# Down product with 25 instead of 18 units of seven products, and with its side work at positions written out in tables

## The chip, the cores and the metric

The kernel runs on one core of a Trainium2 chip. The metric is the device time of one execution in microseconds; the median of several executions is compared. PE is TensorE, DVE VectorE, ACT ScalarE, POOL GpSimd, SP SyncE (it only issues DMAs here).

## The reference

A decoder trunk of two layers over 256 tokens of width 2048, in float32: each layer is an attention part (layer 0: windowed attention with sinks and stick-breaking attention side by side; layer 1: dilated attention) and then a SwiGLU part, each with RMS norm in front and a residual behind. The part at issue is the last line of the SwiGLU:

```python
def swiglu(h, w_gate, w_up, w_down):
    return (jax.nn.silu(h @ w_gate) * (h @ w_up)) @ w_down
```

with `w_gate`, `w_up` of 2048 x 5632 and `w_down` of 5632 x 2048. The product with `w_down` is the **down product**; it runs twice, once for each layer.

## The kernel before

**Splitting.** A float32 product is made of three PE matmuls in a rounded format: both sides are split into a high and a low part, and `three` (L2049) issues high x high, high x low and low x high. ACT makes the high part of a piece of weights (`split`, L1303: `w_hi`, a rounded copy of `raw`), DVE the low part (`split`, L1615: `w_lo` = `raw` - `w_hi`). The prepared pieces ("halves") live in a ring of four slots (`SPLIT` = 4): ACT may write half h+4 only when PE has used half h. The walk through the program gives, on step h, PE its half h, ACT the split of half h+3 and DVE the split of half h+2 (`AHEAD` = 3), and then the other work of that step, in the order in which it is written.

**Eights and sevens.** The down product takes the 44 contraction tiles of 128 in 22 pairs, in two passes over 1024 output columns each (`p` = 0, 1). A pair is a block product of 2 x 2 blocks (two tiles by two halves of the tokens, against two tiles by two column groups of 512). As an "eight" it is done plainly: 8 block products, 24 matmuls of 512 columns, in two halves of 12. As a "seven" it is done after Strassen and Winograd with 7 block products, 21 matmuls, in four parts of 6, 3, 6 and 6 matmuls (`seven_part`, L2055). For that it needs sums of weights (`make_sums`, L1625: three DVE instructions, of 1024, 512 and 512 columns) and forms of the activations (`make_forms`, L1994: four DVE instructions of 128 columns in three steps; `form_high`, L1592, on ACT; `form_low`, L2017, on DVE). Its four parts take splits of 1024, 512, 1024 and 1024 columns ("two", "one", "sums_a", "sums_b"). At the end of a pass, or behind its last seven, the accumulators are mixed on DVE.

**Staging.** The activations of each pair are themselves split into `stage_hi` (ACT, `stage_high`, L1597) and `stage_lo` (DVE, `stage_low`, L1988), 512 columns each, in a ring of four pairs (`STAGED`). In the profile these tiles appear under the names `xT_hi` and `xT_lo`, because they are views of them; the forms appear as `silu_g`.

**Order.** `down` (L824) walks the halves of a pass. Which pairs are sevens stands in `DOWN_SEVENS` (L49): pairs 7, 11, 14, 18, 21 in the first pass and 9, 12, 15, 18 in the second, in both layers. On each step, after the split and after the work of `first_pass` or `second_pass` (mixing the last gate/up block, two transposed blocks for `hT`, the residual, and in layer 0 two early transposes of x), the forms of a seven are made 6, 5 and 4 steps ahead of it, the sums 5, 4 and 3 ahead, `form_high` 3 and `form_low` 2 ahead. A pair is staged on a step of an eight, when `following` (L851) permits it, ACT in front of the forms and DVE behind them; ACT's part waits until PE has used the half before. In the first pass the halves are counted 0 to 53; in the second they go on from there.

**Loads.** SP loads the two tiles of a pair by two DMAs of 512 KB into one of four slots of `raw` (`pair_chunk`, L1057), as soon as DVE's splits have freed it, and between them it issues the transposing DMA of `words` to `wordsT` for the last blocks of the hidden activations.

Of the kernel before, what the change touches and what calls it, by code (L numbers as in the profile page):

```python
# [48 lines left out]
DOWN_SEVENS = ((7, 11, 14, 18, 21), (9, 12, 15, 18))  # L49
DOWN = tuple(tuple("seven" if q in at else "last" if (p, q) == (1, DOWN_PAIRS - 1) else "eight"  # L50
                   for q in range(DOWN_PAIRS)) for p, at in enumerate(DOWN_SEVENS))
# [61 lines left out]
class Counts:  # L113


    def __init__(self):
# [10 lines left out]
        self.form = Count()  # L127
        self.taken = Count()
# [121 lines left out]
def decoder_kernel(nc, widths, x_in, attn_norm, ffn_norm, even_w_in, even_q_norm, even_k_norm, even_sinks,  # L250
# [16 lines left out]
    for name, width in widths.items():  # L267
# [7 lines left out]
    HALVES = 4 + 8 * 8 + 2 * 4 * 8 + 3 * CG * 8 + 2 * (2 * 8 + (FB - 1) * len(RING)  # L275
                                                    + sum(len(PARTS[of]) for half in DOWN for of in half))
    assert DOWN_PAIRS == FK // 2 and DOWN[0][-1] == "seven" and FB % 2
# [3 lines left out]
    with ExitStack() as ctx:  # L281
# [33 lines left out]
        down_forms = silu_g[:, 0, :].rearrange("p (c q) -> p c q", q=P)  # L315
# [194 lines left out]
        def walk(eng, e):  # L510
# [184 lines left out]
            def feed_forward(layer):  # L695
# [50 lines left out]
                def stage_high(q):  # L746
                    e.stage_high(q)

                def stage_low(q):
                    e.stage_low(q)  # L750
                    n.kt.c += 1

# [64 lines left out]
                def staged_first(p):  # L817
                    words_of(p)
                    if p in (18, 19):
                        (stage_high, stage_low)[p - 18](0)  # L820

                starts = [sum(len(PARTS[v]) for v in DOWN[0][:q]) for q in range(DOWN_PAIRS)]

                def down(p, events):  # L824


                    of, sevens, x0 = DOWN[p], DOWN_SEVENS[p], n.x.c
                    begin = [sum(len(PARTS[v]) for v in of[:q]) for q in range(DOWN_PAIRS)]
                    kinds = [kind for v in of for kind in PARTS[v]] + AHEAD * ["pair" if p == 0 else "plain"]
                    for q, what in enumerate(of):  # L830
                        for i in range(len(PARTS[what])):
# [19 lines left out]
                            following = n.kt.c - DOWN_PAIRS * (2 * layer + p)  # L851
                            stages = what != "seven" and following <= q + 1 + i and p * DOWN_PAIRS + following < 2 * DOWN_PAIRS
                            if stages:
                                stage_high(following % DOWN_PAIRS)
                            for v in sevens:
                                to = h - begin[v]
                                if to in (-6, -5, -4):
                                    e.down_forms(to + 6, v)
                                if to in (-5, -4, -3):
                                    since = begin[v] - 2 - max([begin[u] + len(PARTS["seven"]) for u in sevens if u < v], default=0)  # L860
                                    make_sums(to + 5, since, -to - 3)
                                if to == -3:
                                    e.form_high()
                                if to == -2:
                                    e.form_low()
                                    n.form.c += 1
                            if stages:
                                stage_low(following % DOWN_PAIRS)
                        n.taken.c += 1

                def first_pass(q, h, after):
# [4 lines left out]
                    part = h - starts[q]  # L876
# [28 lines left out]
                down(0, first_pass)  # L905
                down(1, second_pass)
# [134 lines left out]
        def _(sp):  # L1041
# [105 lines left out]
            def feed_forward(layer):  # L1147
# [24 lines left out]
                for k in range(FIRST_K, len(BLOCK)):  # L1172
                    joint_pair(before, k, 2 * (slice((FB - 1) * NB, FB * NB),))
                rest = [(q, of, [slice((2 * p + w) * NB, (2 * p + w + 1) * NB) for w in range(2)])
                        for p in range(2) for q, of in enumerate(DOWN[p])]
# [126 lines left out]
        def _(act):  # L1302
# [294 lines left out]
            def stage_high(q):  # L1597
# [16 lines left out]
        def _(dve):  # L1614
# [373 lines left out]
            def stage_low(q):  # L1988
                s = 2 * (e.n.kt.c % STAGED)
                dve.wait_ge(shi_ready, e.n.kt.value(1))  # L1990
# [319 lines left out]
```

## Time and profile before

| | |
|---|---|
| median of 3 runs | 2085.0 us (2084.95 to 2085.22) |
| the profiled execution | 2084.39 us, its span 2082.6 us |
| PE busy | 2076.8 us, 9673 matmuls |
| DVE busy | 1728.3 us |
| ACT busy | 1452.7 us |
| down product, layer 0 | from 780.2 us |
| down product, layer 1 | 1845.6 to 2078.8 us |

The span reaches from the first to the last instruction of one profiled execution; the difference to the execution's own time lies outside it. A busy time is the union of an engine's instructions: matmuls overlap in the pipeline (a matmul of 512 columns is shown with 389 ns, but they start every 0.2265 us), and the same holds, much less, for DVE and ACT. The granted clock of PE was 1.00 over the whole span.

### The profile page before, as it was taken

What the parts mean: (1) busy time and instruction counts of PE and PEld (TensorE: products, weight loads), DVE (VectorE), ACT (ScalarE), POOL (GpSimd) and SP (SyncE); (2) the same over time, 40 slices, a digit from 0 to 9 for tenths busy, and PEclk for the clock granted to TensorE, in tenths of its full rate; (3) what the DMA queues carried; (4) which work ended last, traced back from release to release, by engine and by line L of the source; (5) the groups of instructions that cost most, each with busy time, mean ns of one, the idle gap of its engine ahead of it and who ended that gap; (6) DMA issues with size and microseconds to landing.
All of it is one profiled execution on the core that took longest, in us unless ns stands there. A gap on an engine that the chain in (4) does not pass through costs nothing.

```text
span 2082.6 us, 28699 instructions
## 1 busy us (share of the span) xinstructions
PE 2076.8 (100%) x9673; PEld 1715.1 (82%) x9673; DVE 1728.3 (83%) x2297; ACT 1452.7 (70%) x1972; POOL 100.0 (5%) x79
## 2 busy tenths in 40 slices
PE   9999999999999999999999999999999999999999
PEld 8888888888888888888888888888888888888887
DVE  5776658899999998889767677777999999988888
ACT  6677657677877776656657677666787787777654
POOL 1111000000000000000011101000000000000000
PEclk9999999999999999999999999999999999999999
DMA  8776557787888786665667768676788788876654
GB/s 285 218 224 191 177 167 216 219 260 243 234 256 252 234 230 212 208 210 182 207 212 231 239 210 247 221 225 219 234 242 253 242 234 249 257 224 194 210 195 142
DMA packets 340216, 463.67 MB, mean 223 GB/s; under 512 B 134576, under 2 KB 137360, under 8 KB 340112
## 3 DMA queue, kind: packets, MB, share of 16 engines
q1 hardware_dynamic: 333936, 441.31, 66.2%
q0 software_dynamic: 6080, 20.99, 6.2%
q8 instruction: 60, 0.98, 0.2%
q14 instruction: 44, 0.36, 0.0%
q10 hardware_dynamic: 96, 0.03, 0.0%
HBM read 408.27 MB, written 2.10 MB: 197 GB/s over the span
## 4 chain that ended last, share of the span: by engine, by line
PE 98%; DMA 1%; ACT 1%; DVE 1%; issue 0%; SPq 0%; ACTq 0%; POOLq 0%
PE work L2051 16%; PE work L2053 16%; PE work L2052 16%; PE acc L2051 16%; PE acc L2052 15%; PE acc L2053 15%; PE work L2232 1%; PE work L2270 1%; DMA low_b<-raw 1%; PE work L2182 0%; PE work L2243 0%; ACT w_hi L1320 0%; PE work L2277 0%; DVE w_lo L1622 0%; DMA ident<-in_consts_dram 0%; PE work L2246 0%
## 5 line engine op out<-in xcount | busy, mean ns | idle before, releaser
L1622 DVE TENSOR_TENSOR w_lo<-raw,w_hi 128x1024 fp32r<-128x1024 f32 x716 | 812.0, 1148 | 84.3 <-ACT w_hi L1320 79.1
L1320 ACT ACTIVATE w_hi<-raw 128x1024 fp32r<-128x1024 f32 x716 | 697.5, 995 | 255.5 <-PE work L2053 158.5
L2051 PE MATMUL work<-w_hi,xT_hi 128*128 128x512 f32 x1236 | 481.2, 389 | 0.0
L2053 PE MATMUL work<-w_hi,xT_lo 128*128 128x512 f32 x1236 | 480.9, 389 | 0.0
L2052 PE MATMUL work<-w_lo,xT_hi 128*128 128x512 f32 x1236 | 480.8, 389 | 0.0
L2051 PE MATMUL acc<-w_hi,xT_hi 128*128 128x512 f32 (+1 forms) x898 | 349.7, 389 | 0.6 <-DVE w_lo L1622 0.5
L2053 PE MATMUL acc<-w_hi,xT_lo 128*128 128x512 f32 (+1 forms) x898 | 346.3, 386 | 0.0
L2052 PE MATMUL acc<-w_lo,xT_hi 128*128 128x512 f32 (+1 forms) x898 | 346.2, 386 | 0.0
L1320 ACT ACTIVATE w_hi<-sums 128x1024 fp32r<-128x1024 f32 x196 | 205.7, 1058 | 185.0 <-PE work L2053 138.9
L2053 PEld LDWEIGHTS work<-w_hi,xT_lo 128*128 128x128 f32 x1236 | 232.0, 188 | 48.2
L2052 PEld LDWEIGHTS work<-w_lo,xT_hi 128*128 128x128 f32 x1236 | 232.1, 188 | 48.2
L2051 PEld LDWEIGHTS work<-w_hi,xT_hi 128*128 128x128 f32 x1236 | 232.0, 188 | 48.1
L1622 DVE TENSOR_TENSOR w_lo<-sums,w_hi 128x1024 fp32r<-128x1024 f32 x196 | 236.1, 1221 | 32.5 <-ACT w_hi L1320 32.4
L2051 PEld LDWEIGHTS acc<-w_hi,xT_hi 128*128 128x128 f32 x898 | 168.7, 188 | 38.6 <-DVE w_lo L1622 2.4
L2053 PEld LDWEIGHTS acc<-w_hi,xT_lo 128*128 128x128 f32 x898 | 168.7, 188 | 34.4
L2052 PEld LDWEIGHTS acc<-w_lo,xT_hi 128*128 128x128 f32 x898 | 168.8, 188 | 32.8
L1640 DVE TENSOR_TENSOR sums<-sums,raw 128x512 f32<-128x512 f32 x196 | 134.9, 688 | 3.5
L1635 DVE TENSOR_TENSOR sums<-raw 128x1024 f32<-128x1024 f32 x98 | 119.5, 1220 | 2.0
L2051 PE MATMUL acc<-w_hi,form_hi 128*128 128x512 f32 x294 | 114.4, 389 | 0.0
L2052 PE MATMUL acc<-w_lo,form_hi 128*128 128x512 f32 x294 | 114.4, 389 | 0.0
L2053 PE MATMUL acc<-w_hi,form_lo 128*128 128x512 f32 x294 | 114.4, 389 | 0.0
L2051 PE MATMUL acc<-w_hi,oT_hi 128*128 128x512 f32 x256 | 100.7, 393 | 0.0
(203 smaller groups left out, 2399.2 us busy)
## 6 DMA issues: line engine op xcount, KB each, us to landing
raw<-in_ffn_w_down_dram SPq DMA_DIRECT2D x176, 512.0 KB, 4.8
raw<-in_ffn_w_gate_dram SPq DMA_DIRECT2D x160, 512.0 KB, 4.4
raw<-in_ffn_w_up_dram SPq DMA_DIRECT2D x160, 512.0 KB, 5.2
raw<-in_odd_w_in_dram SPq DMA_DIRECT2D x48, 1024.0 KB, 5.8
raw<-in_even_w_in_dram SPq DMA_DIRECT2D x32, 1024.0 KB, 5.8
raw<-in_even_w_out_dram SPq DMA_DIRECT2D x16, 1024.0 KB, 5.1
raw<-in_odd_w_out_dram SPq DMA_DIRECT2D x16, 1024.0 KB, 6.9
low_a<-raw POOLq DMA_DIRECT2D x20, 512.0 KB, 5.8
```

The costliest lines, as they stand in the source:

```text
L1320: act.activation(w_hi[:, s, 0:out], src, ACT.Copy).then_inc(hi_ready, 1)
L1622: dve.tensor_tensor(w_lo[:, s, 0:out], src, w_hi[:, s, 0:out].bitcast(F32), ALU.subtract).then_inc(lo_ready, 1)
L1635: dve.tensor_tensor(sums[:, 2:4, :], chunk[:, 1:3, :], chunk[:, 0:1, :].broadcast_to([P, 2, NB]), ALU.add).then_inc(sums_made, 1)
L1640: dve.tensor_tensor(sums[:, out, :], a, b, ALU.add).then_inc(sums_made, 1)
L2051: pe.matmul(out_ps, x_hi, wh, start=start, stop=False)
L2052: pe.matmul(out_ps, x_hi, wl, start=False, stop=False)
L2053: return pe.matmul(out_ps, x_lo, wh, start=False, stop=stop)
L2232: last = pe.matmul(o[rows[b], m, :], v_nat[:, k, h * HD:(h + 1) * HD], pt[:, b, (k + m) * P:(k + m + 1) * P], start=first, stop=stop)
L2270: last = pe.matmul(banks[:, b, lo:hi], qT[rows[b], j % 4, m * P:(m + 1) * P], kT[rows[b], key, 0:hi - lo], start=True, stop=True)
```

## The change

The sevens become a table for each layer: 7 and 5 in layer 0, 7 and 6 in layer 1. The step of every staging, form and sum is read from three tables (`STAGE_AT`, `FORM_AT`, `SUM_AT`), whose numbers are steps counted through both passes. `jobs` replaces the rules in `down`; there forms and sums come first and staging last on both engines. Staging waits for exactly the activations of its pair and for the release of its own slot. The forms of the second pass are written to the tile `words` instead of `silu_g`, after a wait for the last transposition of `words`. PE's counter of the forms it waits for becomes its own (`unit`).

```diff
@@ -46,9 +46,26 @@
...
-DOWN_SEVENS = ((7, 11, 14, 18, 21), (9, 12, 15, 18))
-DOWN = tuple(tuple("seven" if q in at else "last" if (p, q) == (1, DOWN_PAIRS - 1) else "eight"
-                   for q in range(DOWN_PAIRS)) for p, at in enumerate(DOWN_SEVENS))
+DOWN_SEVENS = (((5, 8, 11, 14, 16, 18, 21), (9, 11, 13, 15, 18)), ((5, 8, 11, 14, 16, 18, 21), (5, 8, 11, 13, 15, 18)))
+STAGE_AT = (((0, 1, 3, 5, 7, 9, 14, 15, 17, 22, 23, 25, 30, 31, 33, 38, 39, 44, 45, 50, 51, 53, 58, 59, 61, 63, 65,
+            67, 69, 71, 73, 75, 80, 81, 86, 87, 92, 93, 98, 99, 101, 106, 107), (0, 1, 3, 5, 7, 9, 14, 15, 17, 22,
+            23, 25, 30, 31, 33, 38, 39, 44, 45, 50, 51, 53, 58, 59, 61, 63, 65, 67, 69, 71, 73, 75, 80, 81, 86, 87,
+            92, 93, 98, 99, 101, 106, 107)), ((0, 1, 3, 5, 7, 9, 14, 15, 17, 22, 23, 25, 30, 31, 33, 38, 39, 44, 45,
+            50, 51, 53, 58, 59, 61, 63, 65, 67, 72, 73, 75, 80, 81, 83, 88, 89, 94, 95, 100, 101, 103, 108, 109), (0,
+            1, 3, 5, 7, 9, 14, 15, 17, 22, 23, 25, 30, 31, 33, 38, 39, 44, 45, 50, 51, 53, 58, 59, 61, 63, 65, 67,
+            72, 73, 75, 80, 81, 83, 88, 89, 94, 95, 100, 101, 103, 108, 109)))
+FORM_AT = (((8, 8, 8, 8, 8), (12, 13, 14, 15, 16), (20, 21, 22, 23, 24), (28, 29, 30, 31, 32), (34, 35, 36, 37, 38),
+           (40, 41, 42, 43, 44), (48, 49, 50, 51, 52), (70, 71, 72, 73, 74), (76, 77, 78, 79, 80), (82, 83, 84, 85,
+           86), (88, 89, 90, 91, 92), (96, 97, 98, 99, 100)), ((8, 8, 8, 8, 8), (12, 13, 14, 15, 16), (20, 21, 22,
+           23, 24), (28, 29, 30, 31, 32), (34, 35, 36, 37, 38), (40, 41, 42, 43, 44), (48, 49, 50, 51, 52), (62, 63,
+           64, 65, 66), (70, 71, 72, 73, 74), (78, 79, 80, 81, 82), (84, 85, 86, 87, 88), (90, 91, 92, 93, 94), (98,
+           99, 100, 101, 102)))
+SUM_AT = (((5, 6, 7), (13, 14, 15), (21, 22, 23), (29, 30, 31), (35, 36, 37), (41, 42, 43), (49, 50, 51), (71, 72,
+          73), (77, 78, 79), (83, 84, 85), (89, 90, 91), (97, 98, 99)), ((5, 6, 7), (13, 14, 15), (21, 22, 23), (29,
+          30, 31), (35, 36, 37), (41, 42, 43), (49, 50, 51), (63, 64, 65), (71, 72, 73), (79, 80, 81), (85, 86, 87),
+          (91, 92, 93), (99, 100, 101)))
+DOWN = tuple(tuple(tuple("seven" if q in at else "last" if (p, q) == (1, DOWN_PAIRS - 1) else "eight"
+                         for q in range(DOWN_PAIRS)) for p, at in enumerate(passes)) for passes in DOWN_SEVENS)
...
@@ -312,7 +330,8 @@
         added_lo = (low_a, low_b)
         xs_sum = [of.rearrange("p (t s) -> p t s", t=2) for of in (sums[:, 0, :], sums[:, 1, :], shared[:, 0, :], hid[:, 0, :])]
         forms = [of.rearrange("p (c q) -> p c q", q=P) for of in (sums[:, 2, :], sums[:, 3, :], shared[:, 1, :], hid[:, 1, :])]
-        down_forms = silu_g[:, 0, :].rearrange("p (c q) -> p c q", q=P)
+        down_forms = [of.rearrange("p (c q) -> p c q", q=P) for of in
+                      (silu_g[:, 0, :], words[:, 0, :, :].rearrange("p m n -> p (m n)").bitcast(F32))]
         oT_hi = sb("oT_hi", [P, KT, SEQ], F32R)
         oT_lo = sb("oT_lo", [P, KT, SEQ], F32R)
         q_nat = sb("q_nat", [P, MT, NB], F32)
...
@@ -817,15 +829,44 @@
...
+                starts = [[p * sum(len(PARTS[v]) for v in DOWN[layer][0]) + sum(len(PARTS[v]) for v in DOWN[layer][p][:q])
+                           for q in range(DOWN_PAIRS)] for p in range(2)]
+                units = [(p, q) for p in range(2) for q in DOWN_SEVENS[layer][p]]
+                stage_at, form_at, sum_at = STAGE_AT[layer], FORM_AT[layer], SUM_AT[layer]
+
+                def freed(k, base):
+
+
+                    return base - (10, 6, 4, 0)[k] if k < STAGED else base + sum(starts, [])[k - STAGED + 1]
+
+                def jobs(h, base, raw):
+
+
+                    for u, (p, q) in enumerate(units):
+                        for step in range(3):
+                            if form_at[u][step] == h:
+                                e.down_forms(step, p, q, layer)
+                            if sum_at[u][step] == h:
+                                before = starts[units[u - 1][0]][units[u - 1][1]] + len(PARTS["seven"]) if u else 0
+                                make_sums(step, h + AHEAD - before, raw + 2 * (DOWN_PAIRS * p + q) - n.raw.c)
+                        if form_at[u][3] == h:
+                            e.form_high(p)
+                        if form_at[u][4] == h:
+                            e.form_low(p)
+                            n.form.c += 1
+                    for k in range(1, 2 * DOWN_PAIRS):
+                        if stage_at[0][k - 1] == h:
+                            e.stage_high(2 * DOWN_PAIRS * layer + k, freed(k, base), layer)
+                        if stage_at[1][k - 1] == h:
+                            e.stage_low(2 * DOWN_PAIRS * layer + k, None, layer)
+
+                def down(p, events, base, raw):
+
+
+                    of, sevens = DOWN[layer][p], DOWN_SEVENS[layer][p]
+                    begin = [at - starts[p][0] for at in starts[p]]
...
@@ -848,32 +889,17 @@
...
                             events(q, h, h - begin[sevens[-1]] - len(PARTS["seven"]))
-                            following = n.kt.c - DOWN_PAIRS * (2 * layer + p)
-                            stages = what != "seven" and following <= q + 1 + i and p * DOWN_PAIRS + following < 2 * DOWN_PAIRS
-                            if stages:
-                                stage_high(following % DOWN_PAIRS)
-                            for v in sevens:
-                                to = h - begin[v]
-                                if to in (-6, -5, -4):
-                                    e.down_forms(to + 6, v)
-                                if to in (-5, -4, -3):
-                                    since = begin[v] - 2 - max([begin[u] + len(PARTS["seven"]) for u in sevens if u < v], default=0)
-                                    make_sums(to + 5, since, -to - 3)
-                                if to == -3:
-                                    e.form_high()
-                                if to == -2:
-                                    e.form_low()
-                                    n.form.c += 1
-                            if stages:
-                                stage_low(following % DOWN_PAIRS)
+                            jobs(starts[p][0] + h, base, raw)
                         n.taken.c += 1
+                        if what == "seven":
+                            n.unit.c += 1
...
@@ -1589,17 +1616,17 @@
...
-            def form_high():
+            def form_high(p):
...
-                act.activation(form_hi[:, n.form.slot(len(SEVENS)), :, :], down_forms, ACT.Copy).then_inc(down_fhi, 1)
-
-            def stage_high(q):
-
-                n = e.n
-                s = 2 * (n.kt.c % STAGED)
-                act.wait_ge(hT_ready, n.hT.value(unit=2))
-                act.wait_ge(half_used, n.half.value(-1))
+                act.activation(form_hi[:, n.form.slot(len(SEVENS)), :, :], down_forms[p], ACT.Copy).then_inc(down_fhi, 1)
+
+            def stage_high(k, used, layer):
+
+                q = k % DOWN_PAIRS
+                s = 2 * (k % STAGED)
+                act.wait_ge(hT_ready, 2 * (FB * layer + q // 2 + 1))
+                act.wait_ge(half_used, used)
                 act.activation(stage_hi[:, s:s + 2, :], hT[:, 2 * q:2 * q + 2, :], ACT.Copy).then_inc(shi_ready, 1)
...
@@ -1985,39 +2012,40 @@
...
-            def make_forms(step, q):
-
-
-                n = e.n
+            def make_forms(step, p, q, layer):
...
+                n = e.n
+                of = down_forms[p]
                 made = n.form.value(unit=3)
                 (a0, a1), (b0, b1) = ([hT[:, kt, m * P:(m + 1) * P] for m in range(MT)] for kt in (2 * q, 2 * q + 1))
                 if step == 0:
-                    dve.wait_ge(hT_ready, n.hT.value(unit=2))
+                    dve.wait_ge(hT_ready, 2 * (FB * layer + q // 2 + 1))
                     dve.wait_ge(down_flo, n.form.value())
-                    dve.wait_ge(acc_free[1], n.sets[1].value())
-                    if n.x.c > 3 * JB:
-                        dve.wait_ge(result_ready, MT * (n.x.c - 3 * JB))
+                    if p:
+                        dve.wait_ge(wordsT_loaded, 16 * FB * (layer + 1))
                     else:
-                        dve.wait_ge(x_ready, n.x.value())
-                    dve.tensor_tensor(down_forms[:, 1, :], a1, b1, ALU.subtract)
-                    dve.tensor_tensor(down_forms[:, 2, :], a0, a1, ALU.subtract).then_inc(down_formed, 1)
+                        dve.wait_ge(acc_free[1], n.sets[1].value())
+                    dve.tensor_tensor(of[:, 1, :], a1, b1, ALU.subtract)
+                    dve.tensor_tensor(of[:, 2, :], a0, a1, ALU.subtract).then_inc(down_formed, 1)
                 if step == 1:
                     dve.wait_ge(down_formed, made + 1)
-                    dve.tensor_tensor(down_forms[:, 3, :], down_forms[:, 2, :], b1, ALU.add).then_inc(down_formed, 1)
+                    dve.tensor_tensor(of[:, 3, :], of[:, 2, :], b1, ALU.add).then_inc(down_formed, 1)
                 if step == 2:
                     dve.wait_ge(down_formed, made + 2)
-                    dve.tensor_tensor(down_forms[:, 0, :], b0, down_forms[:, 3, :], ALU.subtract).then_inc(down_formed, 1)
-
-            def form_low():
+                    dve.tensor_tensor(of[:, 0, :], b0, of[:, 3, :], ALU.subtract).then_inc(down_formed, 1)
...
@@ -2071,7 +2099,7 @@
                     if staged is None:
                         pe.wait_ge(flo_ready, layer + 1)
                     else:
-                        pe.wait_ge(down_flo, n.form.value())
+                        pe.wait_ge(down_flo, n.unit.value(1))
                         pe.wait_ge(slo_ready, n.taken.value(1))
                     three(work[2], *fs[0], wh[0], wl[0], False, closes)
                     done = three(work[0], *xs[0][1], wh[1], wl[1], False, closes)
```

## Rows read from the trace of the kernel before

**Rows 1.** The page, parts 1 and 4: busy time by engine; the chain that ended last.

```profile
PE 2076.8 (100%) x9673; PEld 1715.1 (82%) x9673; DVE 1728.3 (83%) x2297; ACT 1452.7 (70%) x1972; POOL 100.0 (5%) x79
...
PE 98%; DMA 1%; ACT 1%; DVE 1%; issue 0%; SPq 0%; ACTq 0%; POOLq 0%
```

**Rows 2.** Waits of PE: engine, line, releaser: us in total, times, longest.

```profile
PE acc L2051 <- DVE w_lo L1622: 0.5, 1, 0.5
```

**Rows 3.** Busy us by window: length, PE, PEld, DVE, ACT, POOL, clock, DMA share, GB/s.

```profile
780.40:896.60 116.20, 116.20 (x514) 96.25 (x513) 98.77 (x124) 79.06 (x98) 0.00 (x0) 1.00 0.67 211
896.60:1013.50 116.90, 116.90 (x526) 96.95 (x525) 103.05 (x131) 71.20 (x90) 0.00 (x0) 1.00 0.61 198
1850.00:1966.00 116.00, 116.00 (x514) 96.07 (x513) 98.58 (x125) 78.88 (x99) 0.00 (x0) 1.00 0.65 205
```

**Rows 4.** Timeline of DVE over a seven and two eights, second pass of layer 0.

```profile
962.04 0.69 DVE L1991 TENSOR_TENSOR xT_lo<-hT,xT_hi 128x512 fp32r<-128x512 f32 x1 [0.73 <-ACT xT_hi L1603]
962.65 1.22 DVE L1622 TENSOR_TENSOR w_lo<-sums,w_hi 128x1024 fp32r<-128x1024 f32 x1
964.24 1.22 DVE L1622 TENSOR_TENSOR w_lo<-sums,w_hi 128x1024 fp32r<-128x1024 f32 x1 [0.38 <-ACT w_hi L1320]
965.63 1.23 DVE L1622 TENSOR_TENSOR w_lo<-raw,w_hi 128x1024 fp32r<-128x1024 f32 x1 [0.16 <-ACT w_hi L1320]
...
968.31 0.28 DVE L2012 TENSOR_TENSOR silu_g<-silu_g,hT 128x128 f32<-128x128 f32 x1
968.51 1.22 DVE L1635 TENSOR_TENSOR sums<-raw 128x1024 f32<-128x1024 f32 x1
969.65 1.22 DVE L1622 TENSOR_TENSOR w_lo<-raw,w_hi 128x1024 fp32r<-128x1024 f32 x1
...
971.59 0.69 DVE L1991 TENSOR_TENSOR xT_lo<-hT,xT_hi 128x512 fp32r<-128x512 f32 x1
972.19 1.22 DVE L1622 TENSOR_TENSOR w_lo<-raw,w_hi 128x1024 fp32r<-128x1024 f32 x1
...
977.68 0.69 DVE L1991 TENSOR_TENSOR xT_lo<-hT,xT_hi 128x512 fp32r<-128x512 f32 x1 [0.73 <-ACT xT_hi L1603]
```

**Rows 5.** Timeline of PE: starts of first-pass half 12 and of the half behind a seven.

```profile
809.43 0.39 PE L2051 MATMUL work<-w_hi,xT_hi 128*128 128x512 f32 x1
...
967.65 0.39 PE L2051 MATMUL work<-w_hi,xT_hi 128*128 128x512 f32 x1
```

**Rows 6.** Timeline of the gate/up stage: start, duration, engine, line, operation, count, idle before.

```profile
477.75 1.82 DVE L1622 TENSOR_TENSOR w_lo<-raw,w_hi 128x1024 fp32r<-128x1024 f32 x2
...
479.02 0.19 PEld L2051 LDWEIGHTS work<-w_hi,form_hi 128*128 128x128 f32 x1 [0.18 <-DVE w_lo L1622]
479.11 0.42 PE L2051 MATMUL work<-w_hi,form_hi 128*128 128x512 f32 x1
```

**Rows 7.** Timeline of ACT, halves 8 to 10 of the first pass, layer 0.

```profile
802.23 1.06 ACT L1320 ACTIVATE w_hi<-raw 128x1024 fp32r<-128x1024 f32 x1 [1.14 <-PE work L2053]
803.20 1.41 ACT L1535 ACTIVATE hT<-wordsT 128x512 uint16<-128x512 uint16 x2
804.95 1.06 ACT L1320 ACTIVATE w_hi<-raw 128x1024 fp32r<-128x1024 f32 x1 [0.34 <-PE work L2053]
805.92 1.39 ACT L1535 ACTIVATE hT<-wordsT 128x512 uint16<-128x512 uint16 x2
807.34 0.63 ACT L1603 ACTIVATE xT_hi<-hT 128x512 fp32r<-128x512 f32 x1
```

**Rows 8.** Timeline of DVE, halves 5 to 8 of the first pass, layer 0.

```profile
795.68 0.69 DVE L1991 TENSOR_TENSOR xT_lo<-hT,xT_hi 128x512 fp32r<-128x512 f32 x1 [0.53 <-ACT xT_hi L1603]
...
801.74 1.22 DVE L1622 TENSOR_TENSOR w_lo<-raw,w_hi 128x1024 fp32r<-128x1024 f32 x1
```

**Rows 9.** Groups by line of DVE, down product of layer 0: count, busy, idle before.

```profile
L1991 DVE TENSOR_TENSOR xT_lo<-hT,xT_hi 128x512 fp32r<-128x512 f32 x43 | 29.6, 689 | 23.4 <-ACT xT_hi L1603 23.4
```

**Rows 10.** The page, part 6: issues, count, size, median us to landing.

```profile
raw<-in_ffn_w_down_dram SPq DMA_DIRECT2D x176, 512.0 KB, 4.8
```

More of the change, by code:

```diff
@@ L127, in __init__ @@
         self.form = Count()
+        self.unit = Count()
         self.taken = Count()
@@ L273, in decoder_kernel @@
     CONSTS = len(widths) - 1 - len(BIG) + 8 + 1
-    HALVES = 4 + 8 * 8 + 2 * 4 * 8 + 3 * CG * 8 + 2 * (2 * 8 + (FB - 1) * len(RING)
-                                                    + sum(len(PARTS[of]) for half in DOWN for of in half))
-    assert DOWN_PAIRS == FK // 2 and DOWN[0][-1] == "seven" and FB % 2
+    HALVES = (4 + 8 * 8 + 2 * 4 * 8 + 3 * CG * 8 + 2 * (2 * 8 + (FB - 1) * len(RING))
+              + sum(len(PARTS[of]) for passes in DOWN for half in passes for of in half))
+    assert DOWN_PAIRS == FK // 2 and all(passes[0][-1] == "seven" for passes in DOWN) and FB % 2
     HIGH, LOW = splits_of_block()
@@ L744, in feed_forward @@
                 n.sets[1].c += 1
-                def stage_high(q):
[L747 to L751, printed above, removed]
                 def take_words(w):
@@ L819, in staged_first @@
                     if p in (18, 19):
[L820 to L828, printed above, removed]
+                        (e.stage_high, e.stage_low)[p - 18](2 * DOWN_PAIRS * layer, n.half.c - 1, layer)
@@ L875, in first_pass @@
                         e.silu(h // 2 - 1)
-                    part = h - starts[q]
+                    part = h - starts[0][q]
                     if part < 2 and q in (HIDDEN_MERGE, HIDDEN_LAST):
@@ L904, in feed_forward @@
                 n.ups_ahead = False
-                down(0, first_pass)
-                down(1, second_pass)
+                base, raw = n.half.c, n.raw.c - (AHEAD - 1)
+                down(0, first_pass, base, raw)
+                down(1, second_pass, base, raw)
                 if layer == 1:
@@ L1174, in feed_forward @@
                 rest = [(q, of, [slice((2 * p + w) * NB, (2 * p + w + 1) * NB) for w in range(2)])
-                        for p in range(2) for q, of in enumerate(DOWN[p])]
+                        for p in range(2) for q, of in enumerate(DOWN[layer][p])]
                 for i, (q, of, cols) in enumerate(rest):
@@ L1986, in up, with stage_low @@
                 last.then_inc(acc_free[acc_set], 1)
-            def stage_low(q):
-                s = 2 * (e.n.kt.c % STAGED)
-                dve.wait_ge(shi_ready, e.n.kt.value(1))
+            def stage_low(k, used, layer):
+                q = k % DOWN_PAIRS
+                s = 2 * (k % STAGED)
+                dve.wait_ge(shi_ready, k + 1)
                 dve.tensor_tensor(stage_lo[:, s:s + 2, :], hT[:, 2 * q:2 * q + 2, :],
                                   stage_hi[:, s:s + 2, :].bitcast(F32), ALU.subtract).then_inc(slo_ready, 1)
-            def make_forms(step, q):
+            def make_forms(step, p, q, layer):
                 n = e.n
+                of = down_forms[p]
                 made = n.form.value(unit=3)
@@ L2000, in make_forms, with form_low @@
                 if step == 0:
[L2001 removed]
+                    dve.wait_ge(hT_ready, 2 * (FB * layer + q // 2 + 1))
                     dve.wait_ge(down_flo, n.form.value())
[L2003 to L2009 removed]
+                    if p:
+                        dve.wait_ge(wordsT_loaded, 16 * FB * (layer + 1))
+                    else:
+                        dve.wait_ge(acc_free[1], n.sets[1].value())
+                    dve.tensor_tensor(of[:, 1, :], a1, b1, ALU.subtract)
+                    dve.tensor_tensor(of[:, 2, :], a0, a1, ALU.subtract).then_inc(down_formed, 1)
                 if step == 1:
                     dve.wait_ge(down_formed, made + 1)
[L2012 removed]
+                    dve.tensor_tensor(of[:, 3, :], of[:, 2, :], b1, ALU.add).then_inc(down_formed, 1)
                 if step == 2:
                     dve.wait_ge(down_formed, made + 2)
[L2015 to L2017 removed]
+                    dve.tensor_tensor(of[:, 0, :], b0, of[:, 3, :], ALU.subtract).then_inc(down_formed, 1)
+            def form_low(p):
                 n = e.n
                 dve.wait_ge(down_fhi, n.form.value(1))
[L2020 removed]
+                dve.tensor_tensor(form_lo[:, n.form.slot(len(SEVENS)), :, :], down_forms[p],
                                   form_hi[:, n.form.slot(len(SEVENS)), :, :].bitcast(F32), ALU.subtract).then_inc(down_flo, 1)
@@ L2062, in seven_part @@
                 else:
-                    f = (n.form.c - 1) % len(SEVENS)
+                    f = n.unit.c % len(SEVENS)
                     his, los = ([t[:, 2 * staged + i, :] for i in range(2)] for t in (stage_hi, stage_lo))
```

2 lines of the change are left out of this document (removed).

## The prediction

> **What bounds the kernel now.** I read the page first, then who made PE wait, then busy time by stage, then single instructions at the fastest point of the down product. The page has PE busy for 2076.8 of 2082.6 us and 98% of the chain that ended last is PE [rows 1]. Of its waits for prepared weights the longest in the whole run is one of 0.5 us [rows 2]. So the time is a count of matmuls: in each first pass of the down product 513 of them fill 116.2 us without a gap [rows 3], one every 0.2265 us. The change can gain by issuing fewer, and lose by making PE wait. The engine that could make it wait is DVE: it is busy 99 to 103 us of each 116 in these passes [rows 3], and ACT only 71 to 79.
>
> The kernel hides how close DVE is, so look at a repeating piece of the old second pass, a seven and two eights, where sums, forms, splits and staging all occur once (962.04 to 977.68) [rows 4]. It lasts 15.64 us, which is PE's 21+24+24 matmuls. DVE has idle stretches of 0.38, 0.16 and 0.73 in it; its work is 14.37. An operation's duration is not its price: w_lo takes 1.22, but the next starts 1.14 after it (968.51 to 969.65); at 512 columns 0.60, at 128 columns 0.20. Only before a wait is the full duration paid; without the three waits the work is 14.37 - 3 x 0.08 = 14.13.
>
> How late may w_lo be? The split of the first half behind the seven starts at 965.63 and ends at 966.86; PE starts on it at 967.65 [rows 4, 5]. In the gate/up stage one arrives just in time: w_lo ends at 477.75 + 1.22 = 478.97, the weight load starts at 479.02, the matmul at 479.11 [rows 6]. So w_lo must end 0.14 before PE's start, and the lead at that point is 0.79 - 0.14 = 0.65.
>
> **What goes.** A seven has 21 matmuls where an eight has 24. Seven more sevens: 7 x 3 x 0.2265 = 4.76 us of PE, all of it on the path. This term is firm: -4.8.
>
> **What comes, on DVE.** A seven costs DVE three 1024-splits and one 512-split, three sums (1024, 512, 512), four small forms, one 512 form_lo and one staging; an eight two splits and one staging (2 x 1.135 + 0.605 = 2.88). So one seven with ONE eight costs 14.13 - 2.88 = 11.25 us of DVE, while PE needs 45 x 0.2265 = 10.19. Where sevens stand every second pair DVE is short by 1.06 us each time; where they stand every third it has 1.5 us to spare. The old tables have no two sevens at distance two. The new ones have nine such places, in four runs: layer 0 (14,16,18) and (9,11,13,15), layer 1 (14,16,18) and (11,13,15).
>
> The first of a run: forms and sums of the next seven fall on the halves of the running one. Behind its first part DVE does two small forms (0.42); the 0.38 idle at 964.24 swallows them. Behind the second part come the first sum (1.14) and a form (0.20), 1.34 in front of the split that in the old trace starts at 965.63. The 0.16 idle and its tail of 0.08 take some; the split ends some 1.1 later against a lead of 0.65: PE waits 0.45. Every further one of the run starts with nothing idle and costs the whole 1.06. Together 4 x 0.45 + 5 x 1.06 = 7.1 us. Ends: 0 if the lead of the ring of four splits were enough everywhere; 9 x (11.50 - 10.19) = 11.8 if every wait-tail stays in and there is no lead.
>
> **What comes, at the start of each down product.** The first seven moves from pair 7 to pair 5, with both form steps for ACT and DVE, all five, on half 8, where ACT also takes a transposed block to hT. Old order on ACT: split at 802.23, hT at 803.20, split at 804.95, hT at 805.92, staging at 807.34 [rows 7]. DVE starts its split on half 8 at 801.74; now three sums (2.35) stand ahead of it, of which the idle 0.53 and its tail at 795.68 take 0.6 [rows 8], so it starts near 803.5 and the forms are ready near 805.6. ACT now has a 512 split at 802.2, hT to 804.2, then waits for the forms until 805.6, form_hi to 806.1, split to 807.1, hT to 808.5, staging to 809.1. DVE waits for that staging, ends it at 809.8, and the split of half 12 behind it ends near 811.0. PE wants it at 809.43 [rows 5], less 0.14: 1.7 us late. Twice: 3.4 us (ends 0 and 5).
>
> **Smaller.** A pair's staging on a step only two halves ahead of its use, with a form and a sum in front (half 24 of either layer, half 72 of layer 1): 0.3 us each as an estimate from the same pitches, 0.9 in sum (ends 0 and 2).
>
> **The exact waits.** Staging on ACT waited for the half just done; now for the pair whose slot it takes. But it stands behind a split that itself waits for the half just done, and the old trace has no idle time of ACT before it worth naming: DVE's 23.4 us of waiting for it in one down product [rows 9] comes from ACT's queue order, which stays. Worth 0 on the path (ends -0.5 and +0.5). The forms of the second pass are written to the words tile instead of silu_g: same operations, same sizes, 0; behind their added wait for the transposed words DVE's splits queue, but that transposition is needed half a pass earlier, so 0. Transfers: sums read a chunk up to five halves before its seven; a chunk's slot is free four pairs ahead (over 20 us), and a down chunk lands in 4.8 us [rows 10], so nothing is late, even with two sevens between; 0, ends 0 and +2. SP issues the same 88 pairs and four transpositions in the same order.
>
> **Sum.** -4.8 + 7.1 + 3.4 + 0.9 = +6.6. The profiled execution has a span of 2082.6 and took 2084.4; with this 2091.0. It lies 0.6 under the median of the runs, 2085.0, so a run should show 2091.6; I take 2091.5.
>
> **A rule against the row.** Start to start the row shows 1.14 behind an operation of 1.22 [rows 4]. The Trainium skill (VectorE: DVE Perf Modes, "The DRAIN you can't avoid") says that the next operation does not start until the pipe of the one before is empty. Charged at full durations, a seven and an eight cost six times 1.22, six times 0.69 and four times 0.28, 12.6 us, and the shortage is 2.4 at nine places. The trace does not agree: at those prices the old piece of seven and two eights would need 15.7 of its 15.64 us, and it shows 1.27 of idle.
>
> **Rivals.**
> (a) The lead swallows it, faster. If DVE's order leaves the ring of four splits more lead than the 0.65 I read at one place (the splits of both halves of an eight are long done when PE reaches them in the old trace), no PE wait arises and the saving stands: 2085.0 - 4.8 = 2080.2. It decides from a lead of about 1.1 at the first and 2.2 at the third place of a run. For it: the old kernel shows no wait in its densest stretch. Against: DVE's total there is 11.25 against 10.19, and a lead is used up once.
> (b) Half of it. The late start (3.4) does not occur, since ACT and DVE overlap better than I have them, or the runs cost half: -4.8 + 3 to 8, that is 2083 to 2088, inside what can't be told from no change.
> (c) Full charge, as in the rule above, a mechanism of this kernel all the same: each DVE operation costs its whole duration once nothing idles. 9 x 2.4 less four leads of 0.65 is 19, with 4.3 for the rest and -4.8: +18.5, 2103.5. Against it the row at 968.51.
> (d) Lateness feeds on itself. ACT's form_hi waits for DVE, and the splits behind it in ACT's queue then start late; PE late frees slots late. If each of 14 places loses 0.5 more: 2098.6. For it: that is what the start of the down product shows by my count; against: in a run DVE never idles, so ACT's delay there costs nothing more.
> The change doing other than it says: the tables hold 12 and 13 sevens, 25, against 18; nothing else of the counts can fail.
>
> **Chances.** My forecast, +4.2 to +9: 0.55. (a) 0.14; (b) 0.21; (c) 0.02; (d) 0.08. A change of this kernel can be told from none from about 0.2%, 4.2 us. Faster is (a) less a little that stays under the bound, 0.13; same is (b) and that, 0.22; slower is the rest, 0.65. Range: down into (a)'s edge, 2081.5, up to half of (d), 2096. The likeliest case's own range is 2089.2 to 2094.5.
>
> **What would show it.** Right: PE has waits for w_lo of about 1.1 us each at nine places, the first of a run shorter, with DVE without idle time between them; one of 1.7 near half 12 of each down product; 21 matmuls fewer; DVE busy (14.13 - 3 x 2.88 = 5.5 per added seven) 16 us more in the down product of layer 0 and 22 in layer 1. Wrong: if PE has no waits there and the span falls by 4.8; if the waits come from ACT or a DMA; if DVE's pitch is not 1.14 where it runs full.

## The result and the profile after

The changed kernel takes 2091.8 us (median of 7 runs, 2091.3 to 2092.2); the kernel before takes 2085.0 beside it (7 runs, 2084.0 to 2085.4). The ratio is 1.0033, interval 1.0023 to 1.0043: slower by about 7 us. The profiled run took 2091.3, its span is 2089.5 against 2082.6: +6.9.

First the page, parts 1 and 4 (busy time by engine; the chain that ended last), against [rows 1].

```profile
PE 2076.0 (99%) x9652; PEld 1710.5 (82%) x9652; DVE 1764.7 (84%) x2367; ACT 1466.6 (70%) x1993; POOL 99.9 (5%) x79
...
PE 91%; DVE 6%; ACT 1%; issue 1%; ACTq 0%; DVEq 0%
```

PE issues 21 matmuls fewer and is busy 0.8 us less, in a span 6.9 longer. DVE is busy 36.4 us more, and its share of the chain went from 1% to 6%: DVE now sets part of the end. PE's waits (us in total, times, longest) say where. This row did not exist before; the single 0.5 of [rows 2] stands in both.

```profile
PE work L2079 <- DVE w_lo L1649: 8.1, 11, 1.3
```

Eleven waits, all for the low part that DVE makes. Here are four of them in PE's timeline (start, duration, line, tiles, idle before). The other seven have the same brackets within 0.04 us: 1880.15 as 810.76; 954.65, 1930.70 and 2032.04 as 861.32; 966.01, 1942.05 and 2043.39 as 872.67.

```profile
810.76 0.50 PE L2079 MATMUL work<-w_hi,xT_hi 128*128 128x512 f32 x1 [1.32 <-DVE w_lo L1649]
811.10 0.40 PE L2080 MATMUL work<-w_lo,xT_hi 128*128 128x512 f32 x1
...
861.32 0.50 PE L2079 MATMUL work<-w_hi,xT_hi 128*128 128x512 f32 x1 [0.31 <-DVE w_lo L1649]
...
872.67 0.50 PE L2079 MATMUL work<-w_hi,xT_hi 128*128 128x512 f32 x1 [0.82 <-DVE w_lo L1649]
...
977.36 0.50 PE L2079 MATMUL work<-w_hi,xT_hi 128*128 128x512 f32 x1 [0.84 <-DVE w_lo L1649]
```

Read the price of a wait from the starts, not from the bracket. Undisturbed matmuls start 0.227 apart while each is shown with 0.39, so they overlap by 0.16. At a wait the bracket leaves out the 0.16 of overlap that is lost, and the matmul behind it is shown with 0.50 and its successor starts 0.34 later (810.76 to 811.10), 0.11 late. So a bracket of 0.31 costs 0.58, one of 0.82 costs 1.09, one of 1.32 costs 1.59. (A further 0.03 or so follows: the ten matmuls behind that start up to 0.007 farther apart than usual.)

Next, DVE over one such period, a seven and an eight of the first pass, layer 0, against [rows 4]:

```profile
861.98 1.22 DVE L1649 TENSOR_TENSOR w_lo<-raw,w_hi 128x1024 fp32r<-128x1024 f32 x1
...
868.80 1.22 DVE L1649 TENSOR_TENSOR w_lo<-sums,w_hi 128x1024 fp32r<-128x1024 f32 x1
870.05 1.23 DVE L1662 TENSOR_TENSOR sums<-raw 128x1024 f32<-128x1024 f32 x1
871.20 0.28 DVE L2040 TENSOR_TENSOR silu_g<-silu_g,hT 128x128 f32<-128x128 f32 x1
871.40 1.22 DVE L1649 TENSOR_TENSOR w_lo<-raw,w_hi 128x1024 fp32r<-128x1024 f32 x1
...
873.34 1.22 DVE L1649 TENSOR_TENSOR w_lo<-raw,w_hi 128x1024 fp32r<-128x1024 f32 x1
```

Neither these rows nor those between have idle time before them. The period is 873.34 - 861.98 = 11.36 us, and PE's is 872.67 - 861.32 = 11.35 where its 45 matmuls need 10.19: PE runs at DVE's pace. Over the whole down product of layer 0 DVE's total wait for staged pairs (behind the second bar) fell, from the 23.4 of [rows 9] to

```profile
L2019 DVE TENSOR_TENSOR xT_lo<-hT,xT_hi 128x512 fp32r<-128x512 f32 x43 | 29.5, 686 | 13.0 <-ACT xT_hi L1630 12.9
```

The start of the down product on ACT and then on DVE, against [rows 7] and [rows 8]:

```profile
802.00 0.63 ACT L1347 ACTIVATE w_hi<-raw 128x512 fp32r<-128x512 f32 x1 [1.06 <-PE work L2081]
...
805.50 0.63 ACT L1622 ACTIVATE form_hi<-silu_g 128x512 fp32r<-128x512 f32 x1 [1.56 <-DVE silu_g L2043]
806.03 1.04 ACT L1347 ACTIVATE w_hi<-sums 128x1024 fp32r<-128x1024 f32 x1
806.98 1.40 ACT L1562 ACTIVATE hT<-wordsT 128x512 uint16<-128x512 uint16 x2
808.24 0.60 ACT L1630 ACTIVATE xT_hi<-hT 128x512 fp32r<-128x512 f32 x1
```

```profile
803.19 1.22 DVE L1649 TENSOR_TENSOR w_lo<-raw,w_hi 128x1024 fp32r<-128x1024 f32 x1
...
808.88 0.69 DVE L2019 TENSOR_TENSOR xT_lo<-hT,xT_hi 128x512 fp32r<-128x512 f32 x1 [1.42 <-ACT xT_hi L1630]
809.49 2.35 DVE L1649 TENSOR_TENSOR w_lo<-sums,w_hi 128x1024 fp32r<-128x1024 f32 x2
```

ACT waits 1.56 for the forms, and the copy into hT at 806.98 (1.26 start to start) stands ahead of the staging at 808.24. DVE waits 1.42 for that staging, so the split for half 12 starts at 809.49, ends at 809.49 + 1.22 = 810.71, and PE starts at 810.76.

The last kind of gap is in no waits row. Around half 24 of the first pass all engines show:

```profile
834.05 0.68 DVE L2019 TENSOR_TENSOR xT_lo<-hT,xT_hi 128x512 fp32r<-128x512 f32 x1
...
834.46 0.39 PE L2081 MATMUL work<-w_hi,xT_lo 128*128 128x512 f32 x1
834.66 1.22 DVE L1649 TENSOR_TENSOR w_lo<-raw,w_hi 128x1024 fp32r<-128x1024 f32 x1
...
834.85 0.19 PEld L2079 LDWEIGHTS work<-w_hi,xT_hi 128*128 128x128 f32 x1 [0.43 <-issue]
834.88 0.47 PE L2079 MATMUL work<-w_hi,xT_hi 128*128 128x512 f32 x1
```

The weight load at 834.85 has "issue" in front of it, and PE starts 0.42 after the matmul before it in place of 0.227. With 0.08 in the matmul behind, 0.27 us is lost (three such places: 834.88, 1904.28, 2000.13). The staging on DVE ends at 834.05 + 0.68 = 834.73, and PE starts 0.15 later; a split that came just in time in [rows 6] ended 0.14 before PE's start.

### The profile page after: what moved, and what is told of

It reads as the page before. It is cut to its first block, busy times and chain, and to the rows that moved or that the text cites. A ratio compares the mean times of both kernels' runs of the same rounds, so it can differ in the third digit from the quotient of the medians.

```text
span 2089.5 us, 28758 instructions
## 1 busy us (share of the span) xinstructions
PE 2076.0 (99%) x9652; PEld 1710.5 (82%) x9652; DVE 1764.7 (84%) x2367; ACT 1466.6 (70%) x1993; POOL 99.9 (5%) x79
## 4 chain that ended last, share of the span: by engine, by line
PE 91%; DVE 6%; ACT 1%; issue 1%; ACTq 0%; DVEq 0%
PE acc L2079 16%; PE acc L2081 15%; PE acc L2080 15%; PE work L2079 14%; PE work L2081 14%; PE work L2080 14%; DVE w_lo L1649 3%; PE work L2260 1%; PE work L2298 1%; DVE sums L1662 1%; DVE xT_lo L2019 1%; ACT w_hi L1347 0%; PE work L2210 0%; DVE sums L1667 0%; PE work L2271 0%
## 5 line engine op out<-in xcount | busy, mean ns | idle before, releaser
L2079 PE MATMUL work<-w_hi,xT_hi 128*128 128x512 f32 x1194 | 466.4, 391 | 8.1 <-DVE w_lo L1649 8.1
L2081 PE MATMUL work<-w_hi,xT_lo 128*128 128x512 f32 x1194 | 464.8, 389 | 0.0
L2080 PE MATMUL work<-w_lo,xT_hi 128*128 128x512 f32 x1194 | 464.7, 389 | 0.0
L1347 ACT ACTIVATE w_hi<-sums 128x1024 fp32r<-128x1024 f32 x210 | 220.6, 1059 | 188.5 <-PE work L2081 142.5
L1649 DVE TENSOR_TENSOR w_lo<-sums,w_hi 128x1024 fp32r<-128x1024 f32 x210 | 252.4, 1219 | 29.6 <-ACT w_hi L1347 29.5
L1667 DVE TENSOR_TENSOR sums<-sums,raw 128x512 f32<-128x512 f32 x210 | 144.3, 687 | 3.5
L1662 DVE TENSOR_TENSOR sums<-raw 128x1024 f32<-128x1024 f32 x105 | 128.1, 1220 | 2.3
L2081 PE MATMUL acc<-w_hi,form_lo 128*128 128x512 f32 x315 | 122.6, 389 | 0.0
L2079 PE MATMUL acc<-w_hi,form_hi 128*128 128x512 f32 x315 | 122.6, 389 | 0.0
L2080 PE MATMUL acc<-w_lo,form_hi 128*128 128x512 f32 x315 | 122.6, 389 | 0.0
```

Source lines behind the costliest of these rows:

```text
L1347: act.activation(w_hi[:, s, 0:out], src, ACT.Copy).then_inc(hi_ready, 1)
L1649: dve.tensor_tensor(w_lo[:, s, 0:out], src, w_hi[:, s, 0:out].bitcast(F32), ALU.subtract).then_inc(lo_ready, 1)
L1662: dve.tensor_tensor(sums[:, 2:4, :], chunk[:, 1:3, :], chunk[:, 0:1, :].broadcast_to([P, 2, NB]), ALU.add).then_inc(sums_made, 1)
L1667: dve.tensor_tensor(sums[:, out, :], a, b, ALU.add).then_inc(sums_made, 1)
L2079: pe.matmul(out_ps, x_hi, wh, start=start, stop=False)
L2080: pe.matmul(out_ps, x_hi, wl, start=False, stop=False)
```

## The experiments

In all four the down products are those of the kernel after apart from the edit shown, and all 53 transposing DMAs of the kernel are plain copies of the same bytes (so the transposition is left out of all four):

```diff
-                sp.dma_start_transpose(n_wordsT[...], n_words[...]).then_inc(n_turned, 16)
+                sp.dma_start(n_wordsT[...], n_words[...]).then_inc(n_turned, 16)
...
```

That changes the stages outside the down products, so beside the whole time I give the length of the two down products together, from the start of ACT's first `shared` from `acc` to the end of DVE's last `x`: 465.4 before, 473.0 after (+7.6), and the sum of PE's gaps (start to start over 0.227, counted from 0.26) less the matmuls saved. For the kernel after that is 11.9 - 4.8 = +7.1; the other 0.5 is the slightly wider spacing behind the waits. The kernel before, run beside the first three, has a median of 2084.7 (27 runs).

**The sevens spread.** 21 of them, all at least three pairs apart, with `STAGE_AT`, `FORM_AT` and `SUM_AT` filled to match:

```diff
-DOWN_SEVENS = (((5, 8, 11, 14, 16, 18, 21), (9, 11, 13, 15, 18)), ((5, 8, 11, 14, 16, 18, 21), (5, 8, 11, 13, 15, 18)))
+DOWN_SEVENS = (((5, 8, 11, 15, 18, 21), (9, 12, 15, 18)), ((5, 8, 11, 15, 18, 21), (5, 8, 11, 15, 18)))
```

> The changed kernel with 21 units, none closer than three pairs to the next: pairs 5, 8, 11, 15, 18, 21 in both first passes, 9, 12, 15, 18 and 5, 8, 11, 15, 18 in the second; the transposing DMAs are plain copies (left out: the transposition), which by an earlier run moves the start of the first down product by about 2 us. Theory (DVE is short where sevens stand every second pair): inside the down products three units more than the old kernel save 3 x 0.68 = 2.0; the start of each costs 1.6 (half 12), three late stagings 0.27 each; the waits of 0.57 and 1.1 are all gone. Net +1.9 over the kernel before in the two down products, against +6.9 of the changed kernel: about 2087 us and what the copies cost elsewhere. Rival (each added seven costs alike, wherever it stands: 6.8 us over 7 units, 0.97 each): +2.9, with waits of PE for w_lo spread over the passes. Rival (the load of DVE is not the cause): waits of about 1.1 stay.

Measured: 2089.9 (11 runs), ratio 1.0025 (1.0016 to 1.0034), down products 467.6 (+2.2). PE's waits:

```profile
PE work L2078 <- DVE w_lo L1648: 2.6, 2, 1.3
PE work L2078 <- DMA low_b<-raw: 2.3, 3, 1.7
```

The nine waits at neighbouring sevens are gone; the two left are half 12 of each down product (1.59 each by the starts). With three late stagings (0.27, 0.27, 0.26) the gaps sum to 4.0, less 2.04 for nine matmuls: +1.9, as expected. The whole time is +5.2 in the runs. In the profiled execution the span is 6.1 longer; of that 2.0 us lie before the first down product and 2.1 between them, with 2.3 of waits for `low_b` in all where the kernel before has 0.3.

**DVE's sums shortened.** All 25 sevens, the first of three sums 128 columns wide in place of 1024, so it leaves out most of that sum:

```diff
+                w = P // 2 if n.narrow else NB
-                    dve.tensor_tensor(sums[:, 2:4, :], ...)
+                    dve.tensor_tensor(sums[:, 2:4, 0:w], ...)
```

> The changed kernel (25 units; plain copies in place of the transposing DMAs, left out: the transposition) with the first sum of each seven in the down product made over 128 of its 1024 columns (left out: the other columns of that sum), so DVE has 0.93 us less for each seven while every queue, wait and matmul stays. Theory: a seven and an eight need 10.3 us of DVE against 10.2 of PE, so the nine waits of 0.57 and 1.1 us go but for 0.3 in sum; half 12 keeps about 1.2 to 1.4 of its 1.6. In the two down products -4.8 + 2.8 + 0.3 = -1.7 against the kernel before, range -3 to 0. Rival (the order of the parts or the ring of four, not DVE's load): the waits keep their size, +5 or more.

Measured: 2084.8 (11 runs), ratio 1.0003 (0.9994 to 1.0012), down products 463.3 (-2.1; the stages outside take 2.0 more in the profiled execution). PE's waits, then DVE behind a seven, at the same place as above:

```profile
PE work L2081 <- DVE w_lo L1650: 1.6, 2, 0.8
```

```profile
868.67 1.22 DVE L1650 TENSOR_TENSOR w_lo<-sums,w_hi 128x1024 fp32r<-128x1024 f32 x1
869.92 0.29 DVE L1664 TENSOR_TENSOR sums<-raw 128x128 f32<-128x128 f32 x1
...
870.34 1.22 DVE L1650 TENSOR_TENSOR w_lo<-raw,w_hi 128x1024 fp32r<-128x1024 f32 x1
```

The split that stood at 871.40 stands at 870.34: with 0.9 us less DVE work a seven, the nine waits vanish although all 25 sevens are there. Only 0.09 at 973.95 is left of them. The gaps at half 24 of both layers are gone too, with no staging moved, so these also hang on DVE's load. Half 12 is left with 1.09 in both, less than the 1.2 to 1.4 expected. The shortened sum takes 0.5 and not 0.9 off it, because DVE then waits 0.34 for ACT's high part of a staged pair (797.14); and 1.09 remains, which the next experiment looks into. Gaps 2.5 less 4.76 is -2.3 (expected -1.7). Form steps on ACT, transfers and semaphore waits are all those of the kernel after, so it is the amount of DVE's work there. One rival is left, since this kernel and the spread one both have plain copies: that the transposing DMAs add to the nine waits. No run has the kernel after with plain copies alone. Against it: half 12 waits 1.59 with the copies as without, and DVE's rows of the kernel after show it without idle time through the whole period.

**The copy into hT and one staging moved.** On top of the spread sevens:

```diff
-HIDDEN_MERGE, HIDDEN_WORDS, HIDDEN_LAST = 4, 8, 12
+HIDDEN_MERGE, HIDDEN_WORDS, HIDDEN_LAST = 6, 8, 12
-STAGE_AT = (((0, 1, 3, 5, 7, 9, 14, 15, 17, 22, 23, 25, ...
+STAGE_AT = (((0, 1, 3, 5, 7, 9, 14, 15, 17, 21, 23, 25, ...
```

> As the kernel with 21 units none closer than three pairs (plain copies in place of the transposing DMAs, left out: the transposition), and two moves: ACT's two pieces of the transposed block for hT on pair 6 (halves 14 and 15) instead of pair 4 (halves 8 and 9), and the staging of pair 10 one half earlier, on half 21. Theory (ACT's queue on half 8, with DVE behind its staging, and a staging two halves ahead of its use): the waits of PE at half 12 (1.6 each) and at half 24 (0.27 each) of both down products go, one of 0.25 in the second pass of layer 1 stays: 3.7 us less than the same kernel without the moves, -1.8 against the kernel before in the down products. Rival (the first seven is late because DVE has three sums and four forms there): the waits at half 12 stay within 0.3, and only 0.5 is won.

Measured: 2087.4 (11 runs), ratio 1.0013 (1.0004 to 1.0022), down products 464.5 (-0.9); 2.5 us under the spread kernel where 3.7 was expected. ACT at the start of the down product, and PE at half 12:

```profile
807.88 0.63 ACT L1621 ACTIVATE form_hi<-silu_g 128x512 fp32r<-128x512 f32 x1 [2.87 <-DVE silu_g L2042]
808.42 1.05 ACT L1346 ACTIVATE w_hi<-sums 128x1024 fp32r<-128x1024 f32 x1
809.37 0.61 ACT L1629 ACTIVATE xT_hi<-hT 128x512 fp32r<-128x512 f32 x1
```

```profile
811.43 0.39 PE L2080 MATMUL acc<-w_hi,xT_lo 128*128 128x512 f32 x1
811.90 0.50 PE L2078 MATMUL work<-w_hi,xT_hi 128*128 128x512 f32 x1
```

The staging now follows form_hi after 1.49 in place of 2.74 (805.50 to 808.24), 1.25 less; half 12's gap falls from 1.59 to 0.35, 1.24 less. That much of it was the copy into hT. The 0.35 left (0.24 between the starts, 0.11 behind) I put down to the forms themselves, for which ACT waits 2.87 us; that is read from the rows, not tested. The rival stated for this run, DVE's sums and forms, is true of a part: the shortened sum above took 0.5 off the same wait. The gap at half 24 is gone, the 0.26 in layer 1's second pass, whose staging was not moved, is still there. Gaps 0.96 less 2.04: its down products are 1.1 us shorter than before's by PE's starts, 0.9 by their length. No whole time shows it: +2.7 in the runs, and +3.8 in the profiled execution's span, with 4.7 outside the down products.

**Staging's subtraction on POOL.** 25 sevens; the 88 subtractions that make the low part of a staged pair go from DVE to POOL:

```diff
+            def stage_low(k, used, layer):
...
+                pool.wait_ge(shi_ready, k + 1)
+                pool.tensor_tensor(stage_lo[:, s:s + 2, :], hT[:, 2 * q:2 * q + 2, :],
+                                   stage_hi[:, s:s + 2, :].bitcast(F32), ALU.subtract).then_inc(slo_ready, 1)
```

> The changed kernel (transposing DMAs replaced by plain copies; left out: the transposition) with stage_low, the low part of each staged pair, moved from DVE to POOL. Theory (DVE short where sevens stand every second pair): a seven and an eight cost DVE 11.25 - 1.2 = 10.05 us against 10.19 of PE, the nine waits of 0.57 and 1.1 us go, and DVE no longer waits for ACT's staging, so the wait at half 12 falls from 1.6 to under 1. If POOL makes a 128x512 subtraction in under 2 us and does not slow DVE: 2085.0 - 4.8 + 1 = 2081 us, range 2080 to 2084. Rival (POOL too slow or in DVE's way): PE waits for the staging or for w_lo, 2090 us or more. Rival (not DVE's load): the waits keep their size, 2090 us or more.

Measured: 2144.0 in one run, 2085.1 before beside it; down products 522.8 (+57.4). The group of POOL's subtractions (count, busy, mean ns, idle) and PE's waits for them (total, times, longest):

```profile
L1326 POOL TENSOR_TENSOR xT_lo<-hT,xT_hi 128x512 fp32r<-128x512 f32 x88 | 205.5, 2342 | 396.2 <-ACT xT_hi L1635 396.2
```

```profile
PE work L2084 <- POOL xT_lo L1326: 35.5, 15, 4.4
```

The timelines show why. Two places in each of which POOL's operation lies over one of DVE:

```profile
1907.61 1.46 POOL L1326 TENSOR_TENSOR xT_lo<-hT,xT_hi 128x512 fp32r<-128x512 f32 x1 [4.59 <-ACT xT_hi L1635]
...
1907.84 1.38 DVE L2045 TENSOR_TENSOR silu_g<-silu_g,hT 128x128 f32<-128x128 f32 x1
...
1912.42 1.62 POOL L1326 TENSOR_TENSOR xT_lo<-hT,xT_hi 128x512 fp32r<-128x512 f32 x1 [3.35 <-ACT xT_hi L1635]
...
1912.82 2.31 DVE L1654 TENSOR_TENSOR w_lo<-raw,w_hi 128x1024 fp32r<-128x1024 f32 x1
```

A DVE form of 0.28 takes 1.38, a split of 1.22 takes 2.31: each is longer by 1.1, near the shortest that a POOL operation takes (1.27). And at three places where DVE runs without a pause, POOL doesn't get in at all. The last of the three, two POOL operations in one row:

```profile
2061.14 8.50 POOL L1326 TENSOR_TENSOR xT_lo<-hT,xT_hi 128x512 fp32r<-128x512 f32 x2 [5.70 <-ACT xT_hi L1635]
...
2066.61 0.68 DVE L1654 TENSOR_TENSOR w_lo<-raw,w_hi 128x512 fp32r<-128x512 f32 x1
...
2068.55 0.77 PE L2084 MATMUL work<-w_hi,xT_hi 128*128 128x512 f32 x1 [3.75 <-POOL xT_lo L1326]
```

DVE's last operation ends at 2066.61 + 0.68 = 2067.29, both of POOL's at 2061.14 + 8.50 = 2069.64, that is 2.35 later: twice 1.17. So, as I read it, neither had begun to get through before DVE stopped. Two more places (851.39 and 1005.96) end the same 2.35 behind DVE's last. The two engines exclude each other for whole operations. The Trainium skill says so (SBUF — State Buffer, "Who interferes with whom"): a DVE operation with two inputs in SBUF contends with a GpSimd operation that reads SBUF, for a shared port that is an exclusive lock. The trace agrees (0.28 became 1.38), and shows POOL kept out for the 5 to 6 us in which DVE did not pause.

The long waits cost once more, in PE's clock (windows: length; PE, PEld, DVE, ACT, POOL busy; granted clock; DMA share; GB/s):

```profile
2060.00:2065.00 5.00, 4.79 (x22) 3.63 (x20) 5.00 (x8) 3.43 (x6) 3.86 (x1) 1.00 0.65 210
2065.00:2070.00 5.00, 1.45 (x4) 1.19 (x5) 2.28 (x3) 0.46 (x1) 4.64 (x2) 0.78 0.87 277
2070.00:2075.00 5.00, 5.00 (x14) 3.92 (x13) 0.00 (x0) 0.89 (x1) 0.00 (x0) 0.54 0.39 143
```

PE waited 3.75 us up to 2068.55; on the mean of the last two windows it was granted 0.78 and 0.54 of 2.4 GHz, so most of the last at the 1.2 GHz level. Fifteen such windows of 5 us in the down products have a granted clock under 1.00 and lose 17.1 us in all by it, an estimate that charges idle time too. The account: 35.5 for the waits, 3.2 in shown waits for w_lo beyond the old 0.5, 23 waits by 0.27 for what the bracket leaves out (6.2), 17.1 for the clock, less 4.8, is 57.2 against 57.4; so close an agreement is partly luck, with an estimate in it (PE's gaps summed directly, those of the lower clock included, are 61.4, less 4.8: +56.6). The rival stated for this run (POOL in DVE's way) holds and the 2081 us expected fails: POOL is no cheaper place for this subtraction, and so this run can't tell what DVE without that load would do. It was one run, but the difference is thirty times what separates runs.

**Not measured.** The new order and the exact waits with the old 18 sevens; the kernels before and after with plain copies and nothing else; the later copy into hT with 25 sevens. So the worth of the exact waits alone, the cost of the plain copies alone, and what an hT copy moved as above would give the full kernel stay open.

## Why the prediction was right, point by point

It said 2091.5 and slower; measured 2091.8. The mechanism is the predicted one. That the number is met within 0.3 is partly luck: the down products cost 1.0 more than the sum has, and 0.7 of it was won outside them, as the last rows show. In the terms of its sum:

| term | predicted | measured |
|---|---|---|
| 21 matmuls | -4.8 | -4.8 (x9673 to x9652) |
| first seven at distance two, 4 places | 0.45 each | 0.58 to 0.59 |
| further ones, 5 places | 1.06 each | 1.09 to 1.13 |
| half 12, twice | 1.7 each | 1.59, 1.60 |
| late stagings, 3 places | 0.3 each | 0.27, 0.27, 0.25 |
| wider spacing behind the waits | none | +0.5 |
| sum, down products | +6.6 | +7.6 |
| before the first and between the two | 0 | -0.7 |
| span | +6.6 | +6.9 |

The prediction has no term for the -0.7. 0.5 of it is one wait that the profiled execution before has at 1807.21, in the gate/up stage (0.26 shown, 0.53 by the starts), and the one after has not; why is open:

```profile
PE work L2051 <- DMA low_b<-raw: 0.3, 1, 0.3
```

- **The bound.** That PE's starts set the end and a matmul is worth 0.2265 held: 21 fewer, with most of the waits taken away by the shorter sums, gave gaps of 2.5 less 4.8, -2.3 net, where the length of the down products fell by 2.1.
- **DVE is short by 1.06 at a distance of two.** Right in place, engine and size. The period is 11.36, not 11.25. The missing 0.1 is a full duration paid before a wait: the first sum starts 1.25 behind the split at 868.80, not 1.14, since it waits for that split to end. The step that mis-sized the waits is the pitch of 11.25 from a piece in which the sum stood behind an operation it needn't wait for. At the first place of a run PE starts 0.47 late, as predicted; the 0.11 of its slower first matmul, which the prediction did not have, makes it 0.58 (worked out, not tested alone).
- **The start of the down product.** The predicted chain ACT 806.1, 807.1, 808.5, 809.1 and DVE's 811.0 came out as 806.03, 806.98, 808.24, 808.75 and 810.71. Moving the hT copy took 1.24 of the 1.59 out of it; so that part of the predicted chain is shown, not only argued.
- **Late stagings.** An estimate that held; those moved a half earlier lost their gap. The prediction didn't say that no waits row would show them.
- **Exact waits: worth 0 on the path.** In the down products nothing is left for them once the gaps and the wider spacing are counted. DVE's wait for staging did fall, from 23.4 to 13.0 us in one down product, where the prediction had it stay. DVE's load is a part of that: with the sums shortened and nothing else changed on ACT it is 18.5. What part the exact waits have was not tested.
- **DVE's busy time**: predicted 16 + 22 more, measured 36.4.
- **The rivals.** (a), a lead that swallows it: in the second place of a run the lead is 0, there is no idle on DVE. (b), half: half 12 came within 0.1 of the count, and the neighbouring sevens cost a little more than counted, not half. (c), full durations: a period would last 12.6, it lasts 11.36; where no wait stands between, the next operation starts 1.14 behind one shown with 1.22 (871.40 was 0.20 behind one of 0.28). The Trainium skill (VectorE: DVE Perf Modes, "The DRAIN you can't avoid") lets the next operation start only when the pipe is empty, and adds that one that is not held starts earlier. The trace agrees with the addition, and with the rule only where a wait stands between (1.25 behind 1.22 at 868.80). (d), lateness feeding on itself: the waits of a run don't grow, 0.86 at 966.01, then 0.84 at 977.36.

## What to carry to other kernels

With an engine at 99%, saved work of it pays only while the others can follow: work out each helper's load per repeating period at the pitch of its densest stretch, start to start, and place the trades where the period has room. Here a seven saves 0.68 us of PE and costs 5.2 of DVE (36.4 / 7); three pairs apart no wait for a split came of it, two apart 1.1, which loses 0.4. Where many small placements act on one queue, sum PE's start-to-start gaps: they gave 11.9 of the 12.4 us lost in the down products (7.6 + 4.8), while the waits row showed 8.1. And compare the stage that was changed by itself: here 0.7 us from other stages hid in the span.

## What was not expected of the hardware

- POOL and DVE exclude each other for whole subtractions: 0.28 became 1.38 and 1.22 became 2.31 on DVE, and a POOL operation of 1.27 at the shortest was shown with up to 8.2, where DVE did not pause.
- A wait costs PE 0.27 us more than shown, 0.16 of overlap and 0.11 behind a first matmul of 0.50 in place of 0.39, and 0.03 or so over the ten matmuls behind.
- A wait of 3.75 us was followed by 5 us at a mean granted clock of 0.54; in the kernel after, whose waits are up to 1.3 us, it was 1.00 over the whole run.
